# Output projection of a decoder block: seven block products in place of eight

## The reference, cut to what matters

```python
y_gla = (o * jax.nn.silu(g_og)) @ w_gla_o[l]                 # (1024, 1024)
y_mla = _mla_attention(...) @ w_mla_o[l]                     # (1024, 1024)
mixed = (jax.nn.sigmoid(gate_a) * y_gla
         + jax.nn.sigmoid(gate_b) * y_mla) @ w_out[l]        # the product that is changed
h = _layernorm(DN_ALPHA * h + mixed, ln1_g[l], ln1_b[l])
u = h @ w_up[l]                                              # what follows it
```

## Time and profile before

| | |
|---|---|
| median of 3 runs | 1760.26 us (1759.72 to 1762.26) |
| the profiled execution's own time | 1762.33 us |
| its span, first to last instruction | 1760.6 us |
| TensorE busy | 1729.1 us, 98% of the span |
| VectorE, ScalarE, GpSimd busy | 59%, 44%, 48% |
| mean granted TensorE clock | 0.996 of full speed |
| chain that ended last | TensorE 84%, VectorE 7%, DMA 3%, ScalarE 2% |

### The profile page before, as it was taken

The page is one execution under the profiler, slowest core; times in us unless marked ns, Lnnn a source line. Parts: engine busy times, 40 slices in busy tenths (PEclk is TensorE's granted clock), DMA queues, the critical chain, the costliest instruction groups (busy, mean ns, idle before and its releaser), DMA issues.

```text
span 1760.6 us, 23560 instructions
## 1 busy us (share of the span) xinstructions
PE 1729.1 (98%) x8432; PEld 1449.6 (82%) x8432; DVE 1031.3 (59%) x1772; ACT 770.4 (44%) x1432; POOL 844.5 (48%) x714
## 2 busy tenths in 40 slices
PE   8999999999999999999999999999999999999998
PEld 6788888889998778788888888778888888888886
DVE  6312411156665477455555535677677776788798
ACT  6534443344554214455553103654444544444442
POOL 6888767551112353233333356688776777400000
PEclk9999999999999999999999999999999999999999
DMA  5433433271542378432343451543344442595333
GB/s 168 143 102 112 127 108 112 78 216 49 114 133 90 105 247 269 128 93 80 123 135 115 161 195 56 179 138 114 114 130 153 150 148 90 187 335 183 96 96 120
DMA packets 234110, 241.78 MB, mean 137 GB/s; under 512 B 39196, under 2 KB 162252, under 8 KB 233996
## 3 DMA queue, kind: packets, MB, share of 16 engines
q1 hardware_dynamic: 196076, 171.85, 31.7%
q10 hardware_dynamic: 37920, 68.43, 11.5%
HBM read 164.47 MB, written 75.77 MB: 136 GB/s over the span
## 4 chain that ended last, share of the span: by engine, by line
PE 84%; DVE 7%; DMA 3%; ACT 2%; issue 2%; POOL 1%; SPq 1%; ACTq 0%; DVEq 0%; POOLq 0%
PE psum_all L1231 24%; PE psum_all L1233 23%; PE psum_all L1232 23%; PE psum_all L1563 2%; DMA ga_st<-d_sga 1%; PE psum_all L1579 1%; PE psum_all L1581 1%; PE psum_all L1580 1%; PE psum_all L1551 1%; PE psum_all L1549 1%; PE psum_all L1552 1%; PE psum_all L1550 1%; PE psum_all L1293 1%; PE psum_all L1548 1%; PE psum_all L1297 1%
## 5 line engine op out<-in xcount | busy, mean ns | idle before, releaser
L1109 POOL CAST w_hi<-w_raw 128x512 fp32r<-128x512 f32 (+3 forms) x78 | 58.5, 749 | 253.7 <-PE psum_all L1233 249.4
L1231 PE MATMUL psum_all<-xT_hi,w_hi 128*128 128x512 f32 x376 | 148.8, 396 | 5.8 <-POOL w_lo L1040 3.4
L1232 PE MATMUL psum_all<-xT_lo,w_hi 128*128 128x512 f32 x376 | 147.1, 391 | 0.0
L1233 PE MATMUL psum_all<-xT_hi,w_lo 128*128 128x512 f32 x376 | 147.0, 391 | 0.0
L1878 DVE TENSOR_TENSOR xp<-psum_all,xp 128x512 f32<-128x512 f32 x18 | 12.4, 690 | 216.6 <-PE psum_all L1233 216.6
L1231 PE MATMUL psum_all<-t_hi,w_hi 128*128 128x512 f32 x352 | 137.4, 390 | 1.5 <-DVE r L2336 0.4
L1232 PE MATMUL psum_all<-t_lo,w_hi 128*128 128x512 f32 x352 | 137.0, 389 | 0.0
L1233 PE MATMUL psum_all<-t_hi,w_lo 128*128 128x512 f32 x352 | 137.0, 389 | 0.0
L1171 POOL TENSOR_TENSOR w_lo<-w_raw,w_hi 128x512 fp32r<-128x512 f32 x88 | 115.0, 1315 | 42.3 <-ACT w_hi L3134 42.2
L1111 POOL TENSOR_TENSOR w_lo<-w_raw,w_hi 128x512 fp32r<-128x512 f32 (+3 forms) x78 | 126.6, 1623 | 6.4
L1125 POOL TENSOR_SCALAR p_sb<-p_sb,small 128x128 f32<-128x128 f32 (+3 forms) x64 | 47.9, 749 | 163.2 <-DVE small L2191 163.2
(11 more groups left out here) (562 smaller groups left out, 5090.1 us busy)
## 6 DMA issues: line engine op xcount, KB each, us to landing
w_raw<-in_w_up_dram SPq DMA_DIRECT2D x44, 512.0 KB, 4.8
fa_raw<-d_f SPq DMA_DIRECT2D x76, 256.0 KB, 2.7
w_raw<-in_w_in_dram SPq DMA_DIRECT2D x36, 512.0 KB, 4.3
d_f<-up_g SPq DMA_DIRECT2D x44, 256.0 KB, 3.5
d_f<-f_sum SPq DMA_DIRECT2D x33, 256.0 KB, 3.0
wd<-in_w_down_dram SPq DMA_DIRECT2D x33, 256.0 KB, 4.8
w_raw<-in_w_out_dram SPq DMA_DIRECT2D x8, 1024.0 KB, 5.4
x_tok<-in_x_dram SPq DMA_DIRECT2D x8, 512.0 KB, 6.6
```

The lines of the kernel that those rows point to most:

```text
L1109: wc.done(nc.gpsimd.tensor_copy(w_hi[b][:, w], src[:, w]))
L1231: pe.matmul(out_ap, ah, bh, start=start and i == 0, stop=False, skip_group_check=more)
L1232: pe.matmul(out_ap, ah, bl, start=False, stop=False, skip_group_check=more)
L1233: last = pe.matmul(out_ap, al, bh, start=False, stop=stop and i == len(terms) - 1, skip_group_check=more)
```

## The change

The 8 steps become 7 products of quarter matrices (Strassen-Winograd). With the four token/inner blocks A11 (near, inner half 0), A12 (near, inner half 1), A21, A22 (far) and the quarters B of `w_out`: S1 = A21 + A22, S2 = S1 - A11, S3 = A11 - A21, S4 = A12 - S2; T1 = B12 - B11, T2 = B22 - T1, T3 = B22 - B12, T4 from T2 and B21. Products in the order P1 = A11 B11, P2 = A12 B21, P5 = S1 T1, P6 = S2 T2, P3 = S4 B22, P7 = S3 T3, P4 = A22 T4. The sums are made in fp32 ahead of the split. P2 accumulates on P1 (banks 4 to 7), P6 on P5 (0 to 3), P3 on both, P4 on P7 (4 to 7); P1 and P5 are copied out by ScalarE before that.

In the loop over the 16 `y_mla` pieces VectorE now also makes the S sums, and splits only A11, A12 and A22:

```diff
+                    if part:
+                        ve.wait_ge(sm["mix_hi"], PARTS[i - 1])
+                        split_lo(part[1][:, :], raw_, part[0][:, :]).then_inc(sm["mix_lo"], 1)
+                    made = (lambda ins: ins.then_inc(so_raw[0], 1)) if k == QK - 1 else vc.done
+                    if f < QK and near:
+                        made(V.tensor_tensor(o_s3[:, k, :], o_near[:, k, :], o_far[:, k, :], ALU.subtract))
+                    elif f >= QK and not near:
+                        made(V.tensor_tensor(o_far[:, k, :], o_far[:, k, :], raw_, ALU.add))
+                        vc.wait()
...
+                        made(V.tensor_tensor(o_near[:, k, :], o_far[:, k, :], o_near[:, k, :], ALU.subtract))
+                    elif f >= QK:
...
+                        made(V.tensor_tensor(o_s4[:, k, :], raw_, o_near[:, k, :], ALU.subtract))
```

VectorE after it (`[:, :, :]` is 2048 elements per partition, `[:, t, :]` 512):

```diff
-            out_rows(0, 0)
-            out_rows(0, 1)
+            def add_row(t, dh, extra):
+                c = slice(dh * HALF, (dh + 1) * HALF)
+                ve.wait_ge(row_in[t], row_from[t] + 16)
+                vc.done(V.scalar_tensor_tensor(h_tok[:, t, c], h_tok[:, t, c], ALPHA, extra, ALU.mult, ALU.add))
...
+            ve.wait_ge(*count(so_hi, 1))
+            split_lo(o_s1l[:, :, :], o_far[:, :, :], o_s1h[:, :, :]).then_inc(so_lo[0], 1)
+            ve.wait_ge(*count(so_hi, 2))
+            split_lo(o_s2l[:, :, :], o_near[:, :, :], o_s2h[:, :, :]).then_inc(so_lo[0], 1)
+            for t in range(QK):
+                ve.wait_ge(*count(p_copied, t + 1))
+                add_row(t, 1, o_far[:, t, :])
+            out_rows("C11")
+            for k in range(QK):
+                ve.wait_ge(*count(so_hi, 3 + k))
+                split_lo(o_a12[k][1][:, :], o_s4[:, k, :], o_a12[k][0][:, :]).then_inc(so_lo[0], 1)
+            ve.wait_ge(*count(so_hi, 7))
+            ve.wait_ge(*count(so_lo, 6))
+            split_lo(o_s3l[:, :, :], o_s3[:, :, :], o_s3h[:, :, :]).then_inc(so_lo[0], 1)
+            for t in range(QK):
+                ve.wait_ge(sm["wo_mm"], 12 + t + 1)
+                V.tensor_tensor(o_v[:, t, :], psum[t], o_far[:, t, :], ALU.add).then_inc(v_made[0], 1)
+                ve.wait_ge(*count(p_copied, QK + t + 1))
+                ve.wait_ge(*count(v_made, t + 1))
+                vc.done(V.tensor_tensor(o_near[:, t, :], o_v[:, t, :], o_near[:, t, :], ALU.subtract))
+                add_row(4 + t, 1, o_v[:, t, :])
+                vc.wait()
+                add_row(4 + t, 0, o_near[:, t, :])
+            vc.wait()
+            out_rows("C12")
+            out_rows("C22", (0, 1, 2))
             rows_affine(0)
...
-            out_rows(1, 0, (0, 1, 2))
+            out_rows("C22", (3,))
             rows_affine(4)
...
             rows_low(7)
-            out_rows(1, 1)
+            out_rows("C21")
```

GpSimd splits slots 0 and 1 as before, then makes the T sums, all 2048 wide, between which ScalarE rounds them (`wt_high`):

```diff
+            landed(2)
+            pool.wait_ge(w_split, W1 + 1)
+            wt_sum(wt_a, wt_raw[:, :], wt_a)
+            wt_low(2, wt_a, 1)
+            landed(3)
+            pool.wait_ge(*count(t_sum, 1))
+            wt_sum(wt_b, wt_b, wt_a)
+            wt_low(3, wt_b, 2)
+            landed(4)
+            wt_sum(wt_raw[:, :], wt_a, wt_raw[:, :])
+            wt_low(4, wt_a, 3)
+            wt_low(5, wt_raw[:, :], 4)
+            landed(6)
...
+            wt_sum(wt_a, wt_a, wt_b)
...
+            pool.wait_ge(*used_at(W1 + 4))
...
+            wc.done(nc.gpsimd.tensor_copy(w_hi[b_last_w][:, :], wt_a))
+            wc.wait()
+            nc.gpsimd.tensor_tensor(w_lo[b_last_w][:, :], wt_a, w_hi[b_last_w][:, :].bitcast(F32), ALU.subtract).then_inc(w_split, 1)
```

ScalarE, after it has issued the 8 loads of `h_tok`:

```diff
+            so_high(o_s1h[:, :, :], o_far[:, :, :], 2)
+            so_high(o_s2h[:, :, :], o_near[:, :, :], 3)
+            ac.wait_ge(*count(so_lo, 1))
+            for t in range(QK):
+                p_copy(o_far[:, t, :], psum[4 + t], 0, t)
+            ac.wait_ge(*count(t_sum, 1))
+            wt_high(2, wt_a)
+            ac.wait_ge(sm["wo_mm"], 8)
+            for k in range(QK):
+                so_high(o_a12[k][0][:, :], o_s4[:, k, :], 4)
+            so_high(o_s3h[:, :, :], o_s3[:, :, :], 1)
+            ac.wait_ge(*count(t_sum, 2))
+            wt_high(3, wt_b)
+            ac.wait_ge(*count(so_lo, 2))
+            for t in range(QK):
+                p_copy(o_near[:, t, :], psum[t], 2, t)
...
+            wt_high(4, wt_a)
+            ac.wait_ge(*count(t_sum, 3))
+            wt_high(5, wt_raw[:, :])
```

TensorE's loop has these waits now (`so_lo` counts the VectorE splits above, `v_made` the four sums `o_v`):

```diff
+                if what in ("P5", "P6", "P3", "P7"):
+                    pe.wait_ge(*count(so_lo, {"P5": 1, "P6": 2, "P3": 6, "P7": 7}[what]))
+                for t in range(QK):
+                    if what == "P2":
+                        pe.wait_ge(*count(p_copied, t + 1))
+                    if what == "P6":
+                        pe.wait_ge(*count(p_copied, QK + t + 1))
+                    if what == "P3":
+                        pe.wait_ge(*count(v_made, t + 1))
+                    if what in ("P7", "P4"):
+                        pe.wait_ge(sm["wo_ev"], t + (9 if what == "P4" else 1))
...
+                    if what == "P7" and t == 2:
                         pe.wait_ge(sm["wo_ev"], 8)
                         pe.wait_ge(sm["ln_n"], 4)
...
+                    if what == "P4" and t == 0:
```

More of the change, by code:

```diff
@@ L7 @@
+import itertools
 from contextlib import ExitStack
@@ L342, in block_kernel @@
         wout = w_out[0].rearrange("(k p) c -> p k c", p=P)
[L343 to L345 removed]
+        WOUT = ("P1", "P2", "P5", "P6", "P3", "P7", "P4")
+        for j, quarter in enumerate(((0, 0), (1, 0), (0, 1), (1, 1), (1, 1), None, (1, 0))):
+            slot(("wout", j), 4, HALF, *([(0, HALF, wout[:, 4 * quarter[0]:4 * quarter[0] + 4, quarter[1] * HALF:(quarter[1] + 1) * HALF])] if quarter else []))
         wup = w_up[0].rearrange("(k p) c -> p k c", p=P)
@@ L746, in block_kernel, with mo_raw, mo_part, count @@
         T2_BANK = (2, 6, 3, 7)
+        def mo_raw(i):
+            f, near = divmod(MO_ORDER[i], 2)
+            if f < QK:
+                return (o_near if near else o_far)[:, f, :]
+            return mx[i % 2][:, :]
+        def mo_part(i):
+            f, near = divmod(MO_ORDER[i], 2)
+            if f < QK:
+                return o_a11[f] if near else None
+            return (o_a12 if near else o_a22)[f - QK]
+        PARTS = list(itertools.accumulate(1 if mo_part(i) else 0 for i in range(16)))
+        so_raw, so_hi, so_lo = (sm["rk_hi"], 2), (sm["gate_in"], 3), (sm["kst3_ok"], 1)
+        t_sum, wt_hi, p_copied, v_made = (sm["sins"], 2), (sm["angs"], 2), (sm["lat_sq"], 5), (w_used, 0)
+        def count(signal, n):
+            return signal[0], signal[1] + n
+        W1 = slot_no[("wout", 0)]
+        wt_a, wt_b = w_raw[wbuf(W1)][:, :], w_raw[wbuf(W1 + 1)][:, :]
         def mo_bank(g):
@@ L1629, in rows_t @@
                 last.then_inc(sm["hT_mm"], 1)
-            for j, (th, dh, part) in enumerate(WOUT):
-                second = j % 2
-                n = need(("wout", j))
-                if th == 0 and dh == 0:
-                    pe.wait_ge(sm["mix_lo"], 16 if part else 8)
-                if j == 2:
-                    pe.wait_ge(sm["mo_ev"], 16)
[L1638 to L1646, removed]
-                                    w_part(n, k, 0, HALF), w_part(n, k, 0, HALF, True)) for k in range(4)],
-                                  start=not second, stop=bool(second))
-                    if second:
-                        last.then_inc(sm["wo_mm"], 1)
-                    elif t % 4 == 3:
-                        last.then_inc(w_used, 1)
-                    if j == 4 and t == 6:
@@ new lines, in out_rows @@
+            def out_rows(what, ts=range(4)):
+                first, landed, th, dh = {"C11": (0, 4, 0, 0), "C12": (4, 16, 0, 1), "C22": (8, 20, 1, 1), "C21": (12, 24, 1, 0)}[what]
+                ends = what in ("C12", "C21")
+                for i in ts:
+                    t = 4 * th + i
+                    c = slice(dh * HALF, (dh + 1) * HALF)
+                    ve.wait_ge(sm["wo_mm"], landed + i + 1)
+                    bk = psum[(0 if what == "C12" else 4) + i]
+                    if what == "C11":
+                        ve.wait_ge(row_in[t], row_from[t] + 16)
+                        V.scalar_tensor_tensor(h_tok[:, t, c], h_tok[:, t, c], ALPHA, bk, ALU.mult, ALU.add).then_inc(sm["wo_ev"], 1)
+                    else:
+                        V.tensor_tensor(h_tok[:, t, c], h_tok[:, t, c], bk, ALU.add).then_inc(sm["wo_ev"], 1)
+                    ve.wait_ge(sm["wo_ev"], first + i + 1)
```

114 lines of the change are left out of this document (84 added, 30 removed).

## The result

| | before | after |
|---|---|---|
| median of 5 runs | 1760.15 us (1759.72 to 1762.26) | 1768.79 us (1766.9 to 1771.31) |
| profiled execution, its span | 1762.33, 1760.6 us | 1768.79, 1767.1 us |
| PE, DVE, POOL busy | 98%, 59%, 48% | 97%, 61%, 48% |
| first projection matmul to the 24 transposes of the seam | 96.08 us | 103.22 us |

The ratio is 1.0047, with a 95% interval of 1.0035 to 1.0058: slower by 0.47%, where 1771.0 was forecast. 48 matmuls are gone and the stage is 7.1 us longer.

A forecast was written before the change was run, and what follows sets the result against it. TensorE bounds the stage; removing one step gives -10.88 us, stalls make the sum +9.4, clock adds 1.3: +10.7, so 1762.3 + 10.7 - 2.1 = 1771.0 us median. Range 1757 to 1779 (8 in 10); the forecast's own 1764 to 1776.

The forecast's parts named there:

- 1 P2: Start of P2: TensorE stalls 3.0 us until ScalarE, behind VectorE's split of S1, copies P1 out.
- 2 P5: Start of P5: no stall, T1's low part ending at 1047.7, 0.2 us before P2 ends.
- 3 P6: Start of P6: stall of 0.9 us, T2's low part ending at 1059.7 and P5 at 1058.8.
- 4 P3, first bank: Start of P3: stall of 3.6 us for the first `o_v`, behind VectorE's splits of S4 and S3.
- 5 P3, later bank: P3's second bank: stall of 8.3 us, second `o_v` queued behind operations waiting for slot 5's low part and T4's sum.
- 6 P7: Transposes inside P7: stall of 1.4 us for the last norm of C12.
- 7 seam: Seam after P4 and both next products: stall of 3.1 us, C21's four rows queued behind VectorE's splits.
- clock, restarts: Slow matmuls at half clock after long stalls: 1.3 us taken, between nothing and 6.4; no term for restarts.
- behind the seam, other: After the seam: work as before, so the shift stays and nothing is added.
- `o_v` 2 before 1077: Sign of being wrong, at P3's second bank: second `o_v` made before 1077 us in the earlier profile's clock.
- second rival: P3's second bank: VectorE's `o_near`, both `add_row` and `o_v` 2 precede slot 5's low part; 8.3 goes, 1761.4 us; chance 0.07.
- first rival: Whole stage: GpSimd and two-SBUF VectorE operations form no line, second `o_v` free at 1063; 1754 us; chance 0.13.

The follow-up runs named there:

- e4: Changed kernel with GpSimd's four T sums on 8 columns instead of 2048, leaving T1 to T4 out of the result: 1758.16 us.
- e10: e9 with the four sums for C12 (`h_tok` with `o_far`) moved from VectorE to GpSimd: 1760.28 us.
- e12: e11 with slot 1's four roundings on ScalarE, its row loads issued later, and S2's rounding behind P1's copies: 1758.77 us.
- e3: Changed kernel with GpSimd's T sums and low parts in four pieces of 512 instead of one of 2048: 1769.86 us.
- e5: Changed kernel with the twelve `o_near` / `h_tok` operations on GpSimd instead of VectorE, C12's rows straight behind the four `o_v`: 1763.47 us.
- e9: e5 with the upper half's affine steps on ScalarE and C21's first two rows between the upper half's low parts on VectorE: 1759.87 us.
- e8: e5 with T sums, rounding and low parts in pieces of 512, and the upper half's four affine steps on ScalarE: 1765.77 us.
- e1: Changed kernel with the four `o_v` ahead of the twelve `o_near` / `h_tok` operations in VectorE's order, those still ahead of C12's rows: 1776.47 us.
- e11: e9 with VectorE's scale of C21's first row moved behind the third row's variance: 1757.38 us.
- e2: Changed kernel with the four `o_v` first and the twelve `o_near` / `h_tok` operations behind C12's rows in VectorE's order: 1773.72 us.

## Why the prediction was right, step by step

The forecast (1771.0 for 1768.8) had the right sign and mechanism. From the stage's first matmul on it said +10.7, and the trace has +9.7. That the two are so near is in part luck: the stalls were forecast at 20.3 us and measured 14.3, and of the 6.0 too much 5.0 came back in terms that I had too small or at nothing (clock, restarts, what lies behind the seam). So each term is held against its row. The 24 transposes of the seam came at 1126.3 in the prediction's clock, ahead of its 1128 to 1131.

| step | predicted | measured |
|---|---|---|
| 1 P2 | 3.0, behind ScalarE's copy | 1.50, behind slot 1's low part |
| 2 P5 | 0 | 2.24, behind slot 2's low part |
| 3 P6 | 0.9 | 0.21 |
| 4 P3, first bank | 3.6, behind `o_v` | 0.45, behind slot 4's low part |
| 5 P3, later bank | 8.3 at the second | 7.32 at the third |
| 6 P7 | 1.4 | none |
| 7 seam | 3.1 | 2.59 |
| clock, restarts | 1.3, 0 | 3.8, 1.6 |
| behind the seam, other | 0 | 0.9 |

**Steps 1 and 2: wrong engine, and part of GpSimd's side was left out.** I had GpSimd take turns at slot 1's pieces only, with S1's split behind the last of them and S2's in the gap behind T1's sum, which I took at 4.6. Both splits came sooner: S1's (1028.41 to 1031.10) held slot 1's last low part, 3.19 where the earlier trace rows have 1.29, and S2's, issued at 1031.02, went ahead of T1's sum, issued at 1032.19, which took 6.65 for 4.6. Without these 2.0 P5 would be about 0.2 late in place of 2.2. e4's 8-column sum of 2.25 shows the same with next to no work of its own, e10 shows that the sums on `h_tok` are not the cause, and in e12, with S2's split out of the way, T1's sum took 4.62 and P5 did not wait. The copy that I had last at P2 was on time. The Trainium skill (SBUF — State Buffer, section "Who interferes with whom") has it both ways: "Issue order, not op shape, decides who blocks." The trace agrees: in both cases, the 2.25 and the 6.65 us, VectorE's split had been issued first.

**Steps 3 and 4: I made VectorE later than it was.** I had its four sums for C12 wait for slot 2's low part and T2's sum. The first stood until T1's sum ended, and all four ran in the 2.03 us in which GpSimd waits for its rounding, so VectorE was through with C11 26.7 us after the stage's first matmul, where I had 37.0. Its splits of S4 and S3 then stood (4.40 and 6.50), and still ended at 1059.2, 1 us ahead of the first `o_v`. Of P6's 0.9 only 0.2 is there, and of P3's 3.6 nothing on `o_v`.

**Step 5: the mechanism right, the place not.** The cause is the one predicted (slot 5's low part holds `o_near`, T4's sum holds `add_row`, the free `o_v` behind them), and the size is 1.0 less. But it is the third `o_v`, not the second. The second was made at 1069.85, or 1073.2 in the prediction's clock (its first matmul is at 1023.1), and `o_v` 2 before 1077 was named there as a sign of being wrong. That it is a matter of turns by whole instructions is shown by e3, where instructions of a quarter cut VectorE's waits to 1.8. That it goes when the sums go is shown by e4. So the second rival's condition was met in full: `o_near`, both `add_row` and `o_v` 2 were issued ahead of slot 5's low part (1070.35). Its result was not, for the next `o_near` and `add_row` met the same two GpSimd instructions, one `t` later. Neither the forecast nor the rival had said that getting ahead by one bank only moves the stall; that 7.32 is near 8.3 owes something to that.

**Step 6** was off by 2.4: the last norm of C12 was there 77.4 us after the first matmul, where I had 79.8, 0.5 ahead of TensorE. **Step 7** was right within 0.5. e5 and e9 show its cause, since with P3's wait gone it was 4.05 (e8 shows that the affine steps are not the cause), and fell to 1.49 when two of the four rows left the queue, and to 0.62 when the scale did.

**The clock** was mis-sized by 2.5. Behind the 7.32 us matmuls came 0.43 apart, as in the earlier trace rows at half clock; I had called this stall covered. At the seam and behind it the granted clock was 0.66 of full over 5 us. e1, with 14.5 us of idle time, had its 16 transposes at 3.65 in place of 1.91.

**The first rival** (no line forms, 1754) is 3.4 us below the best that any of these kernels reached (e11, 1757.4, with much of the line kept off the path).

**Not settled:** what the product's removal would give with no waits at all (10.9 in the stage; e11 has 4.2 of it and 4.4 us of idle time, and the other 2.3 is not placed); and why TensorE waits 0.5 to 1.8 us for a `p_sb` copy of ScalarE 190 to 205 us behind the stage's first matmul in the changed kernel and in nine of the experiments, and neither in the kernel before nor in e1, e3 and e5. Not tried: a kernel in which neither engine has SBUF pairs beside the other, and making the first T sum ahead of the stage, where GpSimd stands idle for 11.5 us.

## What to carry to other kernels

Fewer matmuls pay where the operand sums find an engine that is free for them. Here they did not: the two helpers, each half busy, could not work on SBUF pairs at the same time, and four sums of 4.6 us cost the 10.9 us of the product that they save. Before moving such work, write down for each pair of wide operations which of the two will stand, for how long, and what is queued behind it; then order each engine's queue so that what TensorE waits for (here a PSUM operation of 0.7 us, and a reciprocal of 0.2) never stands behind an operation that may. Look for what comes next when a stall is gone: e1, e2 and e12 each removed one and made another, about as large or larger; in e1 because a stage that ran sooner released another engine's work into the same place.
